# Computing a feed-forward unit's gate times up inside its PSUM banks, and adding a norm's squares up in PSUM

## The reference

```python
def _layer_norm(x, g, b):
    mu = jnp.mean(xf, -1, keepdims=True)
    var = jnp.mean(jnp.square(xf - mu), -1, keepdims=True)
    return ((xf - mu) * lax.rsqrt(var + LN_EPS) * g + b).astype(x.dtype)

def _swiglu(x, w1, w3, w2):
    return (jax.nn.silu(x @ w1) * (x @ w3)) @ w2

def first_block(x, mem, ...):
    for l in range(DEPTH):
        x = _layer_norm(a * x + 0.5 * _swiglu(x, ffn1_w1[l], ffn1_w3[l], ffn1_w2[l]), ln1_g[l], ln1_b[l])
        mix = _token_mixing(x, ...)
        x = _layer_norm(a * x + mix, ln2_g[l], ln2_b[l])
        x = _layer_norm(a * x + _cross_attention(x, mem, ...), ln3_g[l], ln3_b[l])
        x = _layer_norm(a * x + 0.5 * _swiglu(x, ffn2_w1[l], ffn2_w3[l], ffn2_w2[l]), ln4_g[l], ln4_b[l])

def half_ffn(x, g, w1, w3, w2):
    return x + FFN_RES * swiglu(rmsnorm(x, g), w1, w3, w2)

def second_block(x, p, ...):
    for layer in range(DEPTH):
        x = half_ffn(x, ffn_norm[layer, 0], ...)
        x = x + mixer(rmsnorm(x, mix_norm[layer]), ...)      # GLA and RG-LRU, then HGRN2
        x = half_ffn(x, ffn_norm[layer, 1], ...)
        gate = jax.nn.sigmoid(rmsnorm(x, ple_norm[layer]) @ ple_gate[layer])
        x = x + gate * (p[layer] @ ple_proj[layer])
    return rmsnorm(x, final_norm)
```

## Time and profile before

| | before |
|---|---|
| three runs | 2774.19, 2778.98, 2779.32 us |
| median | 2778.98 us |
| span of the profiled execution | 2776.7 us |
| PE busy | 2654.9 us (96%) |
| POOL busy | 2204.3 us (79%) |
| ACT busy | 1491.8 us (54%) |
| DVE busy | 1355.8 us (49%) |

### The profile page before, as it was taken

One profiled execution on the slowest core, in us unless ns is written; L12 is line 12 of the kernel. 1 busy time (PEld: TensorE's weight loads), 2 busy tenths in 40 slices (PEclk: granted clock), 3 DMA queues, 4 the chain that ended last, 5 costly groups with the idle time before them and its releaser, 6 DMA issues. The chain is left out here.

```text
span 2776.7 us, 60567 instructions
## 1 busy us (share of the span) xinstructions
PE 2654.9 (96%) x21312; PEld 2578.5 (93%) x21312; DVE 1355.8 (49%) x2564; ACT 1491.8 (54%) x2317; POOL 2204.3 (79%) x1681
## 2 busy tenths in 40 slices
PE   8999999989999999999999989998999999999997
PEld 8998998989999989998989989988999899898996
DVE  2126535567556555635657453356433633535334
ACT  4445556565555545556555554457545544665444
POOL 8886776858979967776859969977999699767994
PEclk9999999999999999999999999999999999999998
DMA  6554444534545544443535535544555355444552
GB/s 242 184 185 139 149 155 137 175 114 160 187 154 180 184 148 165 152 159 122 175 107 190 181 128 191 181 152 137 188 187 182 130 189 182 156 140 155 186 186 77
DMA packets 123537, 450.49 MB, mean 162 GB/s; under 512 B 13680, under 2 KB 13680, under 8 KB 122992
## 3 DMA queue, kind: packets, MB, share of 16 engines
q1 hardware_dynamic: 121104, 441.43, 47.8%
q10 hardware_dynamic: 2272, 6.82, 0.7%
HBM read 447.14 MB, written 1.05 MB: 161 GB/s over the span
## 5 line engine op out<-in xcount | busy, mean ns | idle before, releaser
L376 POOL TENSOR_TENSOR wl<-raw,wh 128x512 fp32r<-128x512 f32 x836 | 1113.9, 1332 | 552.1 <-ACT wh L1157 448.2
L410 PE MATMUL R<-XHB,wh 128*128 128x256 f32 (+1 forms) x4136 | 1176.4, 284 | 7.1 <-POOL wl L378 3.2
L414 PE MATMUL R<-XHB,wl 128*128 128x256 f32 (+1 forms) x4136 | 1169.0, 283 | 0.0
L413 PE MATMUL R<-XLB,wh 128*128 128x256 f32 (+1 forms) x4136 | 1164.8, 282 | 0.0
L378 POOL TENSOR_TENSOR wl<-raw,wh 128x512 fp32r<-128x512 f32 x836 | 1142.7, 1367 | 0.0
L1157 ACT ACTIVATE wh<-raw 128x1024 fp32r<-128x1024 f32 x765 | 801.5, 1058 | 234.3 <-PE R L410 148.2
L410 PEld LDWEIGHTS R<-XHB,wh 128*128 128x128 f32 x4136 | 781.5, 189 | 13.3 <-issue 4.4
L413 PEld LDWEIGHTS R<-XLB,wh 128*128 128x128 f32 x4136 | 784.5, 190 | 2.0 <-issue 1.2
L414 PEld LDWEIGHTS R<-XHB,wl 128*128 128x128 f32 x4136 | 783.2, 189 | 0.0
L410 PE MATMUL Y<-BH,wh 128*128 128x256 f32 x1408 | 397.9, 283 | 1.7 <-DVE BL L1898 1.4
L414 PE MATMUL Y<-BH,wl 128*128 128x256 f32 x1408 | 396.5, 282 | 0.0
(11 more groups left out here) (412 smaller groups left out, 3268.0 us busy)
## 6 DMA issues: line engine op xcount, KB each, us to landing
raw<-in_stream SPq DMA_DIRECT2D x836, 512.0 KB, 3.3
G<-in_wcmp ACTq DMA_DIRECT2D x2, 1024.0 KB, 5.5
G<-in_mem ACTq DMA_DIRECT2D x2, 1024.0 KB, 7.2
TB<-in_table SPq DMA_DIRECT2D x1, 1312.0 KB, 12.6
X<-in_x SPq DMA_DIRECT2D x2, 512.0 KB, 5.5
out_dram<-X ACTq DMA_DIRECT2D x4, 256.0 KB, 2.2
WS<-in_mix_w ACTq DMA_DIRECT2D x2, 256.0 KB, 5.4
PTS<-in_mix_b ACTq DMA_DIRECT2D x2, 256.0 KB, 5.5
```

The source lines that it names most:

```text
L376: pool.tensor_tensor(wl[:, s, 0:512], raw[:, r, 0:512], wh[:, s, 0:512].bitcast(F32), ALU.subtract)
L410: i = pe.matmul(o, wh[w], hi, start=start, stop=False, skip_group_check=True)
L413: pe.matmul(o, wh[w], lo, start=False, stop=False, skip_group_check=True)
L414: i = pe.matmul(o, wl[w], hi, start=False, stop=stop, skip_group_check=True)
```

## The change

Two things change, and the arithmetic stays the same apart from the order of two factors.

In an FFN unit, a (in the "ln" kind), v and h are no longer written to SBUF tiles. They are written in place into the PSUM bank of `R` in which PE left the gate or the up chunk. ACT's bias and tanh read a there ("ln"), ACT's rounding reads h there, and the subtract into `BL` reads h there. The gate's bank is given back after e, and the up chunk's bank after the subtract, not after the multiply. In the "rms" kind DVE waits for its own v before it makes h.

In a norm, ACT's first pair of squares goes to a PSUM bank (`SQS`, bank 3 of `Y`, or `SQS_GATE`, bank 0, at the entry of the embedding gate). DVE's first two adds are in place in that bank, and the third writes `W8[:, 0:2]`, which PE's sum reads as before.

```diff
+        SQS = Y[:, 3, :].rearrange("p (a t) -> p a t", a=2)
+        SQS_GATE = Y[:, 0, :].rearrange("p (a t) -> p a t", a=2)
...
-            def squared(c):
+            def squared(c, sums=SQS):
...
-                    act.activation(flat(W8[:, c - 1:c + 1, :]), flat(X[:, c - 1:c + 1, :]), ACT.Square).then_inc(x_squared, 1)
+                    to = sums if c == 1 else W8[:, c - 1:c + 1, :]
+                    act.activation(to, X[:, c - 1:c + 1, :], ACT.Square).then_inc(x_squared, 1)
...
                 def rounded(j):
                     from_dve()
-                    give_dve(act.activation(HH[:, j % 2, :], HID[:, j % 2, :], ACT.Copy))
+                    h = R[:, t.n["chunk"] % RING, 0:T]
+                    skip(1)
+                    give_dve(act.activation(HH[:, j % 2, :], h, ACT.Copy))
...
-            def split_hidden(j):
-                h = HID[:, j % 2, :]
+            def split_hidden(j, m, h):
+
                 from_act()
                 give_pe(tt_(HL[:, j % 2, :], h, HH[:, j % 2, :].bitcast(F32), ALU.subtract))
+                dve.sem_inc(bank_taken[m % RING], 1)
...
             def hidden_first(j):
...
-                take(stt(h, e, 0.25, o[:, 0:T], ALU.mult, ALU.mult), m)
-                dve.sem_inc(dve_act, 1)
-                t.up(dve_act)
-                split_hidden(j)
+                h = o[:, 0:T]
+                give_act(stt(h, e, 0.25, h, ALU.mult, ALU.mult))
+                split_hidden(j, m, h)
...
             def hidden_rms(j, opens=False):
...
-                take(tt_(v, o[:, 0:T], S4[:, 0:T], ALU.mult), m)
-                give_act(tt_(h, e, v, ALU.mult))
-                split_hidden(j)
+                h = o[:, 0:T]
+                step(tt_(h, h, S4[:, 0:T], ALU.mult))
+                give_act(tt_(h, h, e, ALU.mult))
+                split_hidden(j, m, h)
...
             def hidden_ln(j, opens=False):
...
-                step(tt_(a, o[:, 0:T], S3[:, 0:T], ALU.mult))
-                take(dve.tensor_copy(b1, o[:, T:T + 1]), m)
-                dve.sem_inc(dve_act, 1)
-                t.up(dve_act)
+                a = o[:, 0:T]
+                step(tt_(a, a, S3[:, 0:T], ALU.mult))
+                give_act(dve.tensor_copy(b1, o[:, T:T + 1]))
...
-                step(stt(e, e, 1.0, a, ALU.add, ALU.mult))
+                take(stt(e, e, 1.0, a, ALU.add, ALU.mult), m)
                 m, o = chunk()
-                tt_(v, o[:, 0:T], S4[:, 0:T], ALU.mult)
-                take(ts_(b3, o[:, T:T + 1], 0.25, None, ALU.mult), m)
-                give_act(stt(h, v, b3, e, ALU.add, ALU.mult))
-                split_hidden(j)
+                h = o[:, 0:T]
+                tt_(h, h, S4[:, 0:T], ALU.mult)
+                step(ts_(b3, o[:, T:T + 1], 0.25, None, ALU.mult))
+                give_act(stt(h, h, b3, e, ALU.add, ALU.mult))
+                split_hidden(j, m, h)
...
-            def squares_added(c):
+            def squares_added(c, sums=SQS):
...
-                    w = flat(W8[:, 0:2, :])
-                    give(tt_(w, w, flat(W8[:, 2 * (c // 2) - 2 if c < 7 else 6:2 * (c // 2) if c < 7 else 8, :]), ALU.add), sq_added)
+                    pair = W8[:, c - 2:c, :] if c < 7 else W8[:, 6:8, :]
+                    give(tt_(sums if c < 7 else W8[:, 0:2, :], sums, pair, ALU.add), sq_added)
```

More of the change, by code:

```diff
@@ L1214, in roots, with piece @@
                 act.activation(y[:, 0:512], v[:, 0:512], ACT.Exp, scale=-0.5).then_inc(o_rstd, 1)
-            def piece(c, gain, hi=XH, shift=None):
+            def piece(c, gain, hi=XH, shift=None, sums=SQS):
                 from_dve()
@@ L1221, in piece @@
                 give_dve(act.activation(hi[:, c, :], X[:, c, :], ACT.Identity, scale=gain(c)))
-                squared(c)
-            def squared(c):
+                squared(c, sums)
+            def squared(c, sums=SQS):
                 if c % 2 == 1:
-                    act.activation(flat(W8[:, c - 1:c + 1, :]), flat(X[:, c - 1:c + 1, :]), ACT.Square).then_inc(x_squared, 1)
+                    to = sums if c == 1 else W8[:, c - 1:c + 1, :]
+                    act.activation(to, X[:, c - 1:c + 1, :], ACT.Square).then_inc(x_squared, 1)
             def pieces(gain, bias=None, load=False, shift=None):
@@ L1261, in gate @@
                         a = o[:, 0:T]
-                        skip(1)
                     else:
                         from_dve()
-                        skip(2)
+                        if kind == "ln":
+                            a = R[:, t.n["chunk"] % RING, 0:T]
+                        skip(1)
                     if kind == "ln":
@@ L1816, in _ @@
                     plain(M[:, c, :])
-                piece(0, gain, BH)
+                piece(0, gain, BH, sums=SQS_GATE)
                 act.wait_ge(y_ready, t.value(y_ready))
-                piece(1, gain, BH)
+                piece(1, gain, BH, sums=SQS_GATE)
                 split_next()
@@ L1893, in _ @@
             tt_, ts_, stt = dve.tensor_tensor, dve.tensor_scalar, dve.scalar_tensor_tensor
[L1895 to L1896 removed]
+            def split_hidden(j, m, h):
                 from_act()
                 give_pe(tt_(HL[:, j % 2, :], h, HH[:, j % 2, :].bitcast(F32), ALU.subtract))
+                dve.sem_inc(bank_taken[m % RING], 1)
             def hidden_first(j):
[L1901 removed]
+                e = EB[:, j % 2, :]
                 from_act()
@@ L1961, in ffn @@
                            **{("round", b): 2 for b in range(RING)}}
+                    if kind == "rms":
+                        per[dve_step] = 4
                     with dve.Fori(0, (FC - 2) // 4) as it:
@@ L1969, in ffn, with piece_of_x @@
                 hidden(FC - 1)
-            def piece_of_x(c, gain, hi=XH, lo=XL):
+            def piece_of_x(c, gain, hi=XH, lo=XL, sums=SQS):
                 from_act()
                 give_pe(stt(lo[:, c, :], X[:, c, :], gain(c), hi[:, c, :].bitcast(F32), ALU.mult, ALU.subtract))
-                squares_added(c)
-            def squares_added(c):
+                squares_added(c, sums)
+            def squares_added(c, sums=SQS):
                 if c in (4, 6, 7):
                     need(x_squared, 2 if c == 4 else 1)
-                    w = flat(W8[:, 0:2, :])
-                    give(tt_(w, w, flat(W8[:, 2 * (c // 2) - 2 if c < 7 else 6:2 * (c // 2) if c < 7 else 8, :]), ALU.add), sq_added)
+                    pair = W8[:, c - 2:c, :] if c < 7 else W8[:, 6:8, :]
+                    give(tt_(sums if c < 7 else W8[:, 0:2, :], sums, pair, ALU.add), sq_added)
             def late_root(eps):
@@ L2060, in add_y @@
                     if c > 0:
-                        piece_of_x(c - 1, gain, hi, lo)
-                piece_of_x(DC - 1, gain, hi, lo)
+                        piece_of_x(c - 1, gain, hi, lo, SQS_GATE)
+                piece_of_x(DC - 1, gain, hi, lo, SQS_GATE)
             def add_chunks(alpha, gain=None, between=None):
```

6 lines of the change are left out of this document (2 added, 4 removed).

## The result

The changed kernel takes 2755.57 us (median of four runs, 2755.13 to 2756.83) against 2777.02 us of the kernel before (four runs, 2774.19 to 2779.32). The ratio is 0.992, 95% interval 0.991 to 0.993: 21 us faster. The direction was right and the size was not: over a quarter of the gain had not been foreseen.

The account below looks back on a forecast made before the run. PE was taken as the bound, busy 2654.9 of 2776.7 us, so DVE counts only where PE waits for it. Terms 3.9 + 1.4 + 3.9 + 2.0 + 4.7 = 15.9 us off the 2779.0 median gave 2763 us, range 2755 to 2776.

Parts of the forecast that it names:

- Openings of the "ln" FFNs: Starts of three FFNs' down products: shorter e, h and subtract on DVE save 3.9 us, at most 6.3.
- Ends of "rms" FFNs: Last units of FFNs: shorter h and subtract remove both PE waits at L410, 1.4 us.
- Entries of the cross attention: Two entries: shorter adds of squares in DVE's queue save 3.9 us of PE's wait, at most 4.7.
- The embedding gate: First layer's gate, at its end: two shorter adds in DVE's chain save 2.0 us, at most 2.3.
- The clock: After the cross entries and the gate: PE's clock stays up, saving 4.7 us; the least certain term.
- three stretches named: Stretches of 3.4 us each after the cross entries and gate, with PE's clock at 0.51, 0.50 and 0.50.
- the first rival: After cross entries and gate, some idle time remains and the clock still falls: 11.2 us gained, 2768 us; chance 0.24.
- sum of all upper bounds: Whole kernel: every term at its most, 6.3 + 1.4 + 4.7 + 2.3 + 4.7 = 19.4 us, giving 2759.6 us.
- allowance for a fast execution: Range's low end: an execution like the fastest of before would lie 4.8 us lower, hence 2755 us.
- The next wait: Openings and gate: POOL or ACT ends them as late as now, clock down; 5.3 us gained, 2774 us; chance 0.13.
- PSUM in PE's way: FFN units: added PSUM traffic slows PE's matmuls; at 2.5 ns each, 2795 us; chance 0.07.
- the change does not do what it says: DVE operations with one PSUM operand still stretch beside POOL, so nothing moves: 2777 to 2779 us; chance 0.06.

Follow-up runs that it names:

- the one with two SBUF inputs: Changed kernel, but ACT's first pair of squares goes to SBUF and each norm's first add reads both operands from SBUF, writing PSUM; 2759.62 us.
- the delays: Changed kernel with one, or three, in-place multiplications by 1.0 of the sums in PSUM at each cross attention entry; 2758.79 us with one, 2764.84 with three.
- the added traffic: Changed kernel with two more in-place multiplications by 1.0 of h in its PSUM bank in each of 160 middle units; 2756.73 us.

## Why the prediction was wrong in size

**Openings of the "ln" FFNs.** Right; 3.9 us forecast, 4.85 measured: the three waits of 2.71, 1.47 and 1.44 us became 0.27, 0.23 and 0.27. DVE's timeline of the first, answering:

```profile
625.41 0.30 DVE L1937 TENSOR_SCALAR S<-S 128x256 f32<-128x256 f32 x1
626.48 0.42 DVE L1939 SCALAR_TENSOR_TENSOR M<-M,R 128x256 f32<-128x256 f32 x1 [0.77 <-ACT M L1271]
...
627.46 0.49 DVE L1944 SCALAR_TENSOR_TENSOR R<-R,BB,M 128x256 f32<-128x256 f32 x1
628.48 0.43 DVE L1903 TENSOR_TENSOR BL<-R,BH 128x256 fp32r<-128x256 f32 x1 [0.52 <-ACT BH L1277]
```

e, h and the subtract take what they were priced at. What the sum left out is the first row. The preparation of S4 took 1.26 us before and 0.30 now:

```profile
631.77 1.26 DVE L1933 TENSOR_SCALAR S<-S 128x256 f32<-128x256 f32 x1
```

It reads one SBUF operand only; it began 0.18 us into a subtract of POOL and ended 0.15 us after it. Nothing of it was changed; it came to lie 0.29 us ahead of POOL's subtract instead. Of its 0.96 us only 0.33 shorten the chain, since e now waits 0.77 us for ACT. The three other waits at L524 (0.2 us each) went as well.

**Ends of "rms" FFNs.** Right: both waits of 0.7 us are gone.

**Entries of the cross attention.** Right; 3.9 forecast, 4.7 measured. The whole wait went, because the piece between the two adds, not changed either, was shortened with them: 1.38 us before (first row), 0.68 now.

```profile
564.47 1.38 DVE L1974 SCALAR_TENSOR_TENSOR XLB<-X,SM,XHB 128x256 fp32r<-128x256 f32 x1
...
561.02 0.70 DVE L1989 TENSOR_TENSOR Y<-Y,W 128x512 f32<-128x512 f32 x1
561.75 0.68 DVE L1981 SCALAR_TENSOR_TENSOR XLB<-X,SM,XHB 128x256 fp32r<-128x256 f32 x1
562.47 0.69 DVE L1989 TENSOR_TENSOR W<-Y,W 128x512 f32<-128x512 f32 x1
```

**The embedding gate.** Too much: 2.0 us of PE's wait forecast, 0.85 measured (2.29 to 1.44). Both adds are shorter by 0.97, but a piece between them, stretched to 1.13 us before, ran into POOL's next subtract as well and took 1.64:

```profile
2166.24 1.64 DVE L1981 SCALAR_TENSOR_TENSOR XLB<-X,SM,XHB 128x256 fp32r<-128x256 f32 x1 [0.17 <-ACT XHB L1222]
...
2172.84 0.39 PE L440 MATMUL R<-XHB,wh 128*128 128x256 f32 x1 [1.44 <-DVE XLB L1981]
```

The same happened at the entry of this gate in both layers, which the forecast had at nothing. The first piece took 0.60 us before (first row) and takes 1.51 now, ACT waits for DVE behind it, and PE's wait for ACT's copy is 3.51 us where it was 3.04:

```profile
2146.92 0.60 DVE L1974 SCALAR_TENSOR_TENSOR BL<-X,SM,BH 128x256 fp32r<-128x256 f32 x1 [4.93 <-ACT BH L1221]
...
2130.25 1.51 DVE L1981 SCALAR_TENSOR_TENSOR BL<-X,SM,BH 128x256 fp32r<-128x256 f32 x1 [5.00 <-ACT BH L1222]
```

**The other norms.** "The adds at other norms take 0.69 already and gain nothing" was wrong: the earlier trace rows gives only the median and the longest, and 12 of the 36 adds were stretched, six of them at other norms (1.65 to 1.67 us). No wait of PE is put down to those six, but two of its waits for POOL stand beside them, one of them this:

```profile
1954.46 0.39 PE L439 MATMUL R<-XHB,wh 128*128 128x256 f32 x1 [0.29 <-POOL wl L378]
```

This one and one of 0.44 us in the next layer are gone in every kernel with the squares in PSUM but one, the one with two SBUF inputs, where two of the four stretched adds stand at these places.

These errors nearly cancel, which is why the idle time came out at 12.0 us where the terms had 11.2. That the sum came so near is in part luck.

**The clock.** This is the first step that failed, a term that was mis-sized: "1.6 + 1.5 + 1.7 = 4.7 us". The reasoning, that the clock comes back where the idle time ahead of it is cut, is right: all three stretches named are gone in every trace of the change, the first rival (the clock stays low) is refuted, the delays bring two of the three back, and the three gave back 4.6 us. What failed is to count those three and no others. To see what the clock gave, I laid the matmuls of two traces beside each other, one by one: the first trace of before and the first of the change, then the second of before and the other two. Of the 11.4, 11.4 and 9.6 us by which PE's busy time is shorter, 9.3, 8.1 and 5.4 lie at matmuls that at least one of the two traces shows at the low clock.

So 1 to 5 us came back at other places. How much of this belongs to the change is not shown. It varies with the execution, the count of low-clock losses does not follow the idle time, and the traced executions flatter the change: the mean granted clock is 0.9845 over 28 executions of before and 0.9866 over 14 of the change, some 6 us of clock, against some 10 us by the same measure between the traced ones. Why a given place falls in one execution and not in another was not settled.

**The matmul behind a wait.** This is the second step that failed, a term that the forecast put at nothing when it priced a wait at its idle time alone. Behind a wait, before (first two rows), and the same place without one, after:

```profile
565.91 0.39 PE L410 MATMUL R<-XHB,wh 128*128 128x258 f32 x1 [1.29 <-DVE XLB L1974]
566.13 0.28 PE L413 MATMUL R<-XLB,wh 128*128 128x258 f32 x1
...
562.69 0.28 PE L411 MATMUL R<-XHB,wh 128*128 128x258 f32 x1
562.81 0.28 PE L414 MATMUL R<-XLB,wh 128*128 128x258 f32 x1
```

Matmuls overlap: each lasts 0.28 us, but the next begins 0.12 us after it, so each adds 0.12 us to PE's busy time. The first one behind a wait lasts 0.39 us and overlaps with none ahead of it: it adds 0.27 us more. In the three pairs of traces, the matmuls at full clock that follow a wait in one of the two and not in the other (17 to 19) account for 2.0, 1.9 and 2.1 us of the busy time that was saved. The last 0.1 to 2.2 us of it lie scattered and are not accounted for.

Together, for the first pair: 12.0 us of idle time where 11.2 was forecast, 9.3 of the clock where 4.7 was, and 2.0 behind the waits where nothing was. The measured time lies below even the sum of all upper bounds, 2759.6 us: neither the other stretches nor the matmuls behind the waits had a bound in it. 2.0 of the 4.0 us are the median of before, now 2777.02 where 2778.98 was known. That the range reaches to 2755 comes from the allowance for a fast execution and not from these terms.

**The other rivals.** The next wait did not take over at the openings (0.8 us left, still put down to the subtract). It did at the embedding gate, but there it was a collision that moved. PSUM in PE's way is refuted by units at the same pace with the added traffic. That the change does not do what it says is refuted by 212 operations without one that stretched.

## What to carry to other kernels

Beside an engine that reads SBUF all the time, give each VectorE operation on a critical chain one PSUM operand: here that cut 0.85 to 0.43 and 1.67 to 0.70 us, where an average over the kernel would have shown DVE at 49% and nothing to gain. Price such a change at the waits of the engine that sets the pace. Add what a wait costs beyond its idle time, the longer first operation behind it (0.27 us each here) and a low clock: here PE's idle time was only half of the gain. Operations that still read twice from SBUF will meet the other engine at new moments, so expect some waits elsewhere to change by half a microsecond either way.

## What the runs showed of the hardware

A VectorE operation that reads its only tensor operand from SBUF can be held up as well: the 0.29 us TENSOR_SCALAR at L1933 took 1.26 us beside a subtract of POOL. Operations in place in PSUM cost about as much as others: 431 to 433 ns for 256 columns (L1926) where the subtract into SBUF takes 425, and 699 for 512 where the add into SBUF takes 692. The fixed price of a PSUM source that the Trainium skill gives in VectorE: DVE Perf Modes, section on the TRN2 errata, is not seen here: in the run with two SBUF inputs, the first add (SBUF and SBUF into PSUM) and the second (PSUM and SBUF into PSUM) both take 699 ns at their quickest. The rule that the prediction paraphrases, in the section "Rules for kernel authors" of the same page of the Trainium skill, reads "Either accept 1× (PSUM src), or copy PSUM→SBUF first if you'll do many ops"; here it was quicker to leave the values in PSUM. ACT's rounding is a little quicker from PSUM, 385 ns (mean of 176) against 418 from SBUF. And PE's clock fell behind two idle stretches of 1.10 and 0.84 us with 0.6 us of work between them, but not behind one of 1.09 us, nor, in four of the twelve traces, behind one of 3.1 us at the beginning of the embedding gate.
